# Second attention of a two-block kernel: the query tiles of a pair of heads in the order 0, 7, 1, 6, 2, 5, 3, 4 instead of 0 to 7

## The chip, the core and the metric

One Trainium2 chip, one core. The metric is the device time of one execution in microseconds (us), the median of three runs. Instructions are issued in program order on each engine: TensorE (PE in the rows, PEld its weight loads), VectorE (DVE), ScalarE (ACT), GpSimd (POOL), and SyncE (SP), which issues most transfers. Engines meet through counting semaphores only.

## The reference, cut to what matters

The program is a chain of two transformer blocks over 1024 tokens of width 1024. The second block's attention is causal, with 8 heads of width 64 and a forget bias:

```python
for i in range(S // Q_BLOCK):            # 8 query tiles of 128 rows
    q_blk = q[:, :, q0:q1]
    k_blk = k[:, :, :q1]                 # keys 0 .. q1: tile i has (i + 1) * 128 columns
    logits = einsum('bhqd,bhkd->bhqk', q_blk, k_blk) * scale
    logits = logits + c[:, :, q0:q1, None] - c[:, :, None, :q1]
    p = softmax(where(mask, logits, -inf))
    outs.append(einsum('bhqk,bhkd->bhqd', p, v_blk))
```

Afterwards the result `b_out` is normalised over its 512 columns by row, put beside the gating result, and multiplied with `w_out`. Query tiles do not depend on one another, so their order is free.

## The kernel before

**Items and batches.** The class `Attention` is used twice. For the second attention (`maps == 1`) its list `items` has 64 entries (head, tile): for each of the four pairs of heads, tiles 0 to 7, and for each tile both heads one after the other. I call the two items of one tile a and b. An item of tile i has (i + 1) * 128 score columns. Its probabilities are turned (transposed) and multiplied with the values in batches of up to four 128-column blocks, so that tiles 0 to 3 have one batch for each item and tiles 4 to 7 have two.

**TensorE** (`pe`, L1511 on). Before an even item n it computes the scores of both items of the next tile, n + 2 and n + 3 (`pe_scores`, L1466, with the causal mask added by L1473). Then for each batch b of item n it turns batch b + 1 (`pe_turn`, L1484) and multiplies batch b (`pe_pv`, L1498). So the last turn of item n + 1 is that of the first batch of item n + 2, and that one waits for the exponentials of n + 2. The scores of a head's item fill two of the eight PSUM banks, banks 0 and 1 for a and 2 and 3 for b; new scores wait until the maxima of the tile before are taken (`max0`). No tile further ahead than the next can therefore be under way.

**VectorE** (`dve`). For each item n: `dve_max(n + 2)` (L1589: scores plus bias into `ex`, with the row maximum, and L1592, its negative), the even batches out of PSUM (`evacuate`, L1540), and `dve_out(n)` (L1610, L1617: the result times one over the row sum).

**ScalarE** (`act`). For each item n: the odd batches out of PSUM, `act_exp(n + 2)` (L1552), and what `act_beside_att2` puts there: squares for the normalisation that follows (L2143). The squares of the attention's own results are taken in the last pair of heads, tile by tile, two items after the tile.

```python
if n + 2 < len(self.items) and (self.wide(n + 2) if self.maps == 2 else n % 2 == 0):
    self.pe_scores(pe, n + 2)
for b in range(self.first[n], self.first[n + 1]):
    ...
    if b + 1 < len(self.batches):
        self.pe_turn(pe, b + 1)
    self.pe_pv(pe, b)
```

**After it.** GpSimd makes a root from each square (`pool_m_root`), VectorE scales tile by tile from 0 to 7 (`dve_m_scale`), TensorE turns the scaled tiles and `pe_out` multiplies them with `w_out`, again from tile 0 to 7.

Of the kernel before, what the change touches and what calls it, by code (L numbers as in the profile page):

```python
# [26 lines left out]
NT = SEQ // P  # L27
# [15 lines left out]
NSLOT = 12  # L43
NRAW = 4
NH1, NH2 = 4, 8
LAM_INIT = 0.8 - 0.6 * math.exp(-0.3 * 0)
NEG = -1.0e30
RSQRT_MAGIC = 0x5F3759DF
# [18 lines left out]
def _program(nc, io, ctx):  # L67
# [3 lines left out]
    def sem(name):  # L71
        if name not in sems:
            sems[name] = ctx.enter_context(nc.semaphore(name))
        return sems[name]
# [447 lines left out]
    def loaded(eng, name, n=1):  # L522
        eng.wait_ge(sem("in_" + name), 16 * n)
# [27 lines left out]
    N1 = NT + 1  # L551
# [827 lines left out]
    class Attention:  # L1379
# [7 lines left out]
        def __init__(self, tag, q, k, v, out, heads, dv, meta, maps, ex, atb, bias=None, neglam=None):  # L1387
            self.tag, self.q, self.k, self.v, self.out = tag, q, k, v, out
            self.heads, self.dv, self.meta, self.maps = heads, dv, meta, maps
            self.ex, self.atb, self.bias, self.neglam = ex, atb, bias, neglam  # L1390
            if maps == 2:
                self.items = [(h, i) for h in range(heads) for i in range(NT)]
            else:

                self.items = [(h, i) for g in range(0, heads, 2) for i in range(NT) for h in (g, g + 1)]
            names = ("s0", "s1", "max0", "max1", "exp0", "exp1", "prob", "turned", "evac0", "evac1", "pv",
                     "o_out")
            self.s = {n: sem(f"{tag}_{n}") for n in names if maps == 2 or n not in ("s1", "max1", "exp1", "prob")}

            self.batches = []  # L1400
            for n, (h, i) in enumerate(self.items):
                full = [(meta + t * P, P, t + (1 if meta else 0)) for t in range(i + 1)]
                tiles = full + ([(0, meta, 0)] if meta else [])
                for b in range(0, len(tiles), 4):
                    self.batches.append((n, tiles[b:b + 4]))
            self.first = {}
            for b, (n, _) in enumerate(self.batches):
                self.first.setdefault(n, b)
            self.first[len(self.items)] = len(self.batches)
            self.beside_long = {b for n in range(len(self.items)) if self.items[n][1] == NT - 3  # L1410
                                for b in self.steps(n)}
# [159 lines left out]
        def dve_max(self, v, n, link):  # L1571
            w = self.ncols(self.items[n][1])
            h = self.items[n][0]
            for m in range(self.maps):
                v.wait_ge(self.s[f"s{m}"], n + 1)
                if n >= 3:
                    v.wait_ge(self.s[f"exp{m}"], n - 2)
                if self.maps == 2:
                    if n >= 3:
                        v.wait_ge(self.s["turned"], self.first[n - 2])  # L1580
                    v.tensor_tensor_reduce(self.ex[:, n % 3, m, 0:w], self.score(n, m, 0, w), maskrow[:, L1 - w:L1],  # L1581
                                           -1.0, 3.0e38, ALU.add, ALU.min, negmax[:, n % 3, m:m + 1])\
                        .then_inc(self.s[f"max{m}"], 1)
                else:
                    if self.items[n][1] == 0:
                        v.wait_ge(tile_in[h], 32)
                    if n >= 3:
                        v.wait_ge(self.s["turned"], self.first[n - 2])
                    link(v.tensor_tensor_reduce(self.ex[:, n % 3, 0, 0:w], self.score(n, 0, 0, w),  # L1589
                                                self.bias[:, h, 0:w], 1.0, -3.0e38, ALU.add, ALU.max,  # L1590
                                                lmax[:, n % 2, 0:1]))
                    v.tensor_scalar(negmax[:, n % 3, 0:1], lmax[:, n % 2, 0:1], -1.0, None, ALU.mult)\  # L1592
                        .then_inc(self.s["max0"], 1)
# [527 lines left out]
    att2 = Attention("att2", q2, k2, v2, o2, NH2, ST, 0, 1, ex2, at2, bias=negc)  # L2121
# [8 lines left out]
    m_sq, m_rooted = sem("turn_m_sq"), t1_rooted  # L2130
# [2 lines left out]

    def act_m_square(act, i, part):

        n = i if part else NT + i
        if n:
            act.wait_ge(m_sq, n)
        if not part:
            act.wait_ge(att2.s["o_out"], len(att2.items) - 2 * NT + 2 * i + 2)  # L2140
        src = au[:, i, :] if part else o2[:, :, i * P:(i + 1) * P]
        junk = junk_m[:, :] if part else junk_m[:, :].rearrange("p (k c) -> p k c", k=4)
        nc.scalar.activation(junk, src, ACT.Square, accum_out=stat[:, i, part:part + 1]).then_inc(m_sq, 1)  # L2143

    def act_beside_att2(act, n):

        if n < 4 * NT and n % 4 == 3:
            act_m_square(act, n // 4, 1)
        last = n - (len(att2.items) - 2 * NT)
        if last >= 3 and last % 2 == 1:  # L2150
            act_m_square(act, (last - 3) // 2, 0)

    def pool_m_root(pool, i, part):
        n = i if part else NT + i
        pool.wait_ge(m_sq, n + 1)
        nc.gpsimd.tensor_scalar(tmpa[:, i, part:part + 1], stat[:, i, part:part + 1], 1.0 / HALF, EPS,
                                ALU.mult, ALU.add).then_inc(root_eps, 1)
        eps_added[0] += 1
        pool.wait_ge(root_eps, eps_added[0])
        nc.gpsimd.tensor_tensor(rst[:, i, part:part + 1], tmpa[:, i, part:part + 1], mhalf[:, 0:1], ALU.pow)\  # L2160
            .then_inc(m_rooted, 1)

    def dve_m_scale(v, i):
        for part in range(2):
            v.wait_ge(m_rooted, N1 + (i if part else NT + i) + 1)
            if i >= 2:
                v.wait_ge(m_turned, 2 * (i - 2) + part + 1)
            if part:
                dst, src, gain = xs_m[:, i % 2, 1, :], au[:, i, :], gb_m[:, 0:HALF]
            else:  # L2170
                dst, gain = (t.rearrange("p (k c) -> p k c", k=4) for t in (xs_m[:, i % 2, 0, :], gb_m[:, HALF:D]))
                src = o2[:, :, i * P:(i + 1) * P]
            v.scalar_tensor_tensor(dst, src, rst[:, i, part:part + 1], gain, ALU.mult, ALU.mult).then_inc(m_scaled, 1)
# [424 lines left out]
    @block.gpsimd  # L2598
    def _(pool):
        pool_in1(pool)  # L2600
        pool.wait_ge(met, 3 * K["ssm"])
        pool_weights(pool, U_GLU, U_O1[1])
        for i in range(NT):
            pool_o_root(pool, i)
        pool_y_sums(pool)
        pool_weights(pool, U_O1[1], U_O1[1] + 4)
        pool_y_root(pool)
        pool_weights(pool, U_O1[1] + 4, N_BLOCK1)
        pool_beside_out(pool, 0, mlp1)
        mlp1.pool(pool)  # L2610
        mlp1.freed(pool, 3)
        pool_weights(pool, N_BLOCK1, N_BLOCK1 + 4)
        mlp1.pool_down_lo(pool, NF - 1)
        mlp1.freed(pool, 5)
        u = N_BLOCK1 + 4
        for i in range(NT + 2):
            for k in range((2, 1, 1)[i] if i < 3 else 0):
                pool_weights(pool, u, u + 1)
                u += 1
            if i < NT:  # L2620
                post[1].pool_root1(pool, i)
            if i >= 2:
                post[1].pool_root2(pool, i - 2)
        mlp1.down_over(pool)
        pool_weights(pool, u, len(stream) - 4)
        for part in (1, 0):
            for i in range(NT):
                pool_m_root(pool, i, part)
        pool_weights(pool, len(stream) - 4, len(stream))
        pool_beside_out(pool, 2, mlp2)  # L2630
        mlp2.pool(pool)
        mlp2.pool_down_lo(pool, NF - 1)
        for i in range(NT):
            post[3].pool_root1(pool, i)
# [86 lines left out]
    def _(act):  # L2721
# [87 lines left out]
        load(act, "gb_m", gb_m[:, 0:HALF], rowb(gains_a))  # L2809
        load(act, "gb_m", gb_m[:, HALF:D], rowb(gains_b))  # L2810
        att2.act(act, act_beside_att2)
        act_m_square(act, NT - 1, 0)
        for i in range(NT + 2):
            if i < NT:
                act_m_hi(act, i)
# [12 lines left out]
    def _(v):  # L2828
# [28 lines left out]
        link(v.tensor_tensor(lamv[:, 4:5], lamv[:, 3:4], lamv[:, 2:3], ALU.subtract))  # L2857
        link(v.tensor_scalar(lamv[:, 4:5], lamv[:, 4:5], -LAM_INIT, None, ALU.add))
        dve_ssm_turned(v, link)
# [9 lines left out]
        loaded(v, "gb_o")  # L2869
        link(v.tensor_scalar(gb_o[:, :], gb_o[:, :], 1.0 - LAM_INIT, None, ALU.mult))  # L2870
        for i in range(2):
# [143 lines left out]
```

## Time and profile before

| what | us |
|---|---|
| median of three runs | 2594.71 (2590.66 to 2598.65) |
| the profiled execution, its own time | 2594.34 |
| its span in the trace | 2592.5 |
| mean granted TensorE clock, share of full | 0.973 |
| TensorE matmuls busy | 2426.4 (94%) |
| VectorE, ScalarE, GpSimd busy | 1474.3, 798.0, 1150.1 |
| second attention, from about 1597 to 1762 | 165 |

The chain of work that ended last is 81% TensorE. The first number of a timeline's row is counted from the start of the span. The ends of matmuls are modelled, and each is longer than the distance to the next, so that a group of matmuls is best measured from its start to the start of the next group.

### The profile page before, as it was taken

To read this page: it belongs to the slowest core of one execution; us is meant where nothing else is said; L and a number is where in the kernel's file an instruction comes from. 1 tells how busy PE (TensorE), PEld (TensorE's weight loads), DVE (VectorE), ACT (ScalarE), POOL (GpSimd) and SP (SyncE) were. 2 spreads that over 40 slices of the span, in tenths; PEclk is the share of its full clock that TensorE was granted. 3 is DMA by queue.
4 is the path that set the end of the run, shared out by engine and by line. 5 is a ranking of instruction groups with operands and counts; after the bars stand their busy time and mean duration, and the time that the engine had idled before them with its cause. 6 is when DMAs were issued, how large, how long until landed. Compare 5 with 4: busy or idle time off the path is not lost.

```text
span 2592.5 us, 32813 instructions
## 1 busy us (share of the span) xinstructions
PE 2426.4 (94%) x11718; PEld 1967.5 (76%) x11718; DVE 1474.3 (57%) x2113; ACT 798.0 (31%) x1517; POOL 1150.1 (44%) x888
## 2 busy tenths in 40 slices
PE   7997877898999999999989998989989999999996
PEld 7976755686788888888768886768768888888885
DVE  5974666537456555655574311664645655555556
ACT  4231355624322222222242002552532222222222
POOL 3220040254555555665583443001745565555553
PEclk9998899898999999999999999999999999999998
DMA  5445520023111111211152113001311111111114
GB/s 144 126 130 132 169 73 1 1 81 122 37 49 49 50 59 49 60 49 49 59 181 67 45 54 106 1 1 41 123 41 58 57 53 49 49 49 50 59 49 146
DMA packets 176915, 179.29 MB, mean 69 GB/s; under 512 B 39704, under 2 KB 139544, under 8 KB 176816
## 3 DMA queue, kind: packets, MB, share of 16 engines
q1 hardware_dynamic: 171520, 164.02, 20.9%
q10 hardware_dynamic: 5296, 13.96, 1.5%
q8 instruction: 60, 0.98, 0.2%
q14 instruction: 39, 0.32, 0.0%
HBM read 147.46 MB, written 30.49 MB: 69 GB/s over the span
## 4 chain that ended last, share of the span: by engine, by line
PE 81%; DVE 8%; ACT 4%; issue 2%; DMA 2%; POOL 2%; SPq 0%; POOLq 0%; ACTq 0%; DVEq 0%
PE ps L267 23%; PE ps L268 23%; PE ps L269 23%; PE ps L1498 3%; PE ps L1466 3%; PE ps L1484 2%; ACT ex L1552 2%; PE ps L474 1%; DVE hbuf L425 1%; DMA msb<-ssm_lags 1%; DVE ex L1603 1%; DVE hbuf L1989 1%; PE ps L2710 1%; PE ps L456 0%; DVE hbuf L431 0%
## 5 line engine op out<-in xcount | busy, mean ns | idle before, releaser
L1989 DVE TENSOR_TENSOR hbuf<-hbuf,ps 128x1024 f32<-128x1024 f32 x320 | 390.7, 1221 | 254.0 <-PE ps L269 232.2
L267 PE MATMUL ps<-mlp_dh,mlp_fh 128*128 128x512 f32 x672 | 264.4, 393 | 12.8 <-POOL mlp_dzl L1790 10.0
L269 PE MATMUL ps<-mlp_dh,mlp_fl 128*128 128x512 f32 x672 | 263.3, 392 | 0.0
L268 PE MATMUL ps<-mlp_dl,mlp_fh 128*128 128x512 f32 x672 | 262.7, 391 | 0.0
L207 POOL TENSOR_TENSOR wgt<-raw,ones 128x512 fp32r<-128x512 f32 x76 | 86.7, 1141 | 328.3 <-PE ps L269 165.1
L1777 POOL TENSOR_TENSOR mlp_s_raw<-mlp_gh_raw,mlp_s_raw 128x512 f32<-128x512 f32 x44 | 57.1, 1299 | 284.1 <-PE ps L269 284.1
L267 PEld LDWEIGHTS ps<-mlp_dh,mlp_fh 128*128 128x128 f32 x672 | 126.6, 188 | 43.7 <-POOL mlp_dzl L1790 10.8
L269 PEld LDWEIGHTS ps<-mlp_dh,mlp_fl 128*128 128x128 f32 x672 | 126.5, 188 | 27.7
L268 PEld LDWEIGHTS ps<-mlp_dl,mlp_fh 128*128 128x128 f32 x672 | 126.7, 189 | 27.5
L1790 POOL TENSOR_TENSOR mlp_dl<-mlp_d_raw,mlp_dh 128x1024 fp32r<-128x1024 f32 x42 | 113.9, 2712 | 46.5 <-ACT mlp_dh L1966 46.5
L1484 PE MATMUL ps<-ident,ex 128*128 128x128 f32 (+1 forms) x464 | 83.0, 291 | 41.6 <-DVE ex L1603 26.6
L2026 DVE TENSOR_TENSOR mlp_fl<-mlp_p,mlp_fh 128x512 fp32r<-128x512 f32 x42 | 114.4, 2725 | 3.6
L1552 ACT ACTIVATE ex<-ex,negmax 128x144 f32<-128x144 f32 (+15 forms) x128 | 99.4, 778 | 33.2 <-DVE negmax L1592 32.4
L1777 POOL TENSOR_TENSOR mlp_s_raw<-mlp_gl_raw,mlp_ul 128x512 f32<-128x512 f32 x44 | 57.2, 1300 | 116.0 <-PE ps L269 116.0
L209 POOL TENSOR_TENSOR wgt<-raw,wgt 128x512 fp32r<-128x512 f32 x76 | 104.1, 1370 | 6.0
L1466 PE MATMUL ps<-k,q 64*128 64x512 f32 (+6 forms) x416 | 89.9, 543 | 10.8 <-DVE negmax L1581 7.5
L1484 PEld LDWEIGHTS ps<-ident,ex 128*128 128x128 f32 (+1 forms) x464 | 52.2, 147 | 56.7 <-DVE ex L1603 34.5
L1589 DVE CUSTOM_DVE_ANT_0 ex<-ps,negc 128x128 f32<-128x128 f32 (+7 forms) x64 | 48.2, 754 | 79.4 <-PE ps L1473 79.1
L267 PE MATMUL ps<-x1h,chunk_w 128*128 128x352 f32 (+2 forms) x256 | 89.1, 348 | 2.6 <-DVE x1l L625 1.8
L1923 ACT CAST mlp_s3h<-mlp_s_raw 128x512 fp32r<-128x512 f32 x44 | 27.3, 621 | 202.7 <-POOL mlp_s_raw L1777 202.7
L269 PE MATMUL ps<-x1h,chunk_w 128*128 128x352 f32 (+2 forms) x256 | 87.5, 342 | 0.0
L268 PE MATMUL ps<-x1l,chunk_w 128*128 128x352 f32 (+2 forms) x256 | 87.4, 341 | 0.0
(485 smaller groups left out, 6719.4 us busy)
## 6 DMA issues: line engine op xcount, KB each, us to landing
h<-hbuf SPq DMA_DIRECT2D x24, 512.0 KB, 2.9
mlp_d_raw<-in_w_down SPq DMA_DIRECT2D x21, 512.0 KB, 3.4
mlp_d_raw<-in_w_ffn_out SPq DMA_DIRECT2D x21, 512.0 KB, 3.6
raw<-in_w_in SPq DMA_DIRECT2D x40, 256.0 KB, 2.8
raw<-in_w_out SPq DMA_DIRECT2D x32, 256.0 KB, 2.7
res_b<-h SPq DMA_DIRECT2D x16, 512.0 KB, 4.4
mlp_ul<-in_w_up SPq DMA_DIRECT2D x22, 256.0 KB, 3.0
mlp_uh_raw<-in_w_up SPq DMA_DIRECT2D x22, 256.0 KB, 3.3
```

The costliest lines, as they stand in the source:

```text
L207: nc.gpsimd.tensor_tensor(wh[:, s, :], r, ones[:, 0:1].broadcast_to([P, 512]), ALU.mult).then_inc(w_hi, 1)
L209: nc.gpsimd.tensor_tensor(wl[:, s, :], r, wh[:, s, :].bitcast(F32), ALU.subtract).then_inc(w_split, 1)
L267: pe.matmul(out, lhs[0], rhs[0], start=first, stop=False, skip_group_check=over)
L268: pe.matmul(out, lhs[0], rhs[1], start=False, stop=False, skip_group_check=over)
L269: return pe.matmul(out, lhs[1], rhs[0], start=False, stop=last, skip_group_check=over)
L1466: mm = pe.matmul(self.score(item, m, a, b), self.q[rows, t, i * P:(i + 1) * P], self.k[rows, t, a:b], start=True, stop=True)
L1484: t = pe.transpose(ps[0:w, self.tbank(b), j * P:(j + 1) * P], self.ex[:, n % 3, 0, c:c + w], ident[:, :])
L1552: nc.scalar.activation(e, e, ACT.Exp, scale=-1.0 if self.maps == 2 else 1.0, bias=negmax[:, n % 3, m:m + 1], accum_out=psum_l[:, n % 3, m: ...
L1777: nc.gpsimd.tensor_tensor(blk[name][2][:, :, :], x[:, :, :], y[:, :, :], op).then_inc(self.s["sums"], 1)
L1790: nc.gpsimd.tensor_tensor(self.d[z][1][:, :], self.d_raw[z][:, :], self.d[z][0][:, :].bitcast(F32), ALU.subtract).then_inc(self.s["split"], 1)
L1989: v.tensor_tensor(self.acc[:, i, :], self.acc[:, i, :], src, ALU.add).then_inc(self.s["added"], 1)
L2026: v.tensor_tensor(self.f[b][1][:, c], src, self.f[b][0][:, c].bitcast(F32), ALU.subtract)\
```

## The change

`items` of the second attention runs over the tiles in the order `ORDER2`; the pairing of heads stays. The rest of the diff keeps counts in step with it: the wait of `dve_max` for a head's bias sits at the first tile in the order (still tile 0), and the squares and roots of the attention's result are made and counted in the new order. The stage after it still goes through tiles 0 to 7.

```diff
+ORDER2 = [0, 7, 1, 6, 2, 5, 3, 4]
@@
-                self.items = [(h, i) for g in range(0, heads, 2) for i in range(NT) for h in (g, g + 1)]
+                self.items = [(h, i) for g in range(0, heads, 2) for i in ORDER2 for h in (g, g + 1)]
@@
-                    if self.items[n][1] == 0:
+                    if self.items[n][1] == ORDER2[0]:
                         v.wait_ge(tile_in[h], 32)
@@ def act_m_square(act, i, part):
-        n = i if part else NT + i
+        n = i if part else NT + ORDER2.index(i)
@@
-            act.wait_ge(att2.s["o_out"], len(att2.items) - 2 * NT + 2 * i + 2)
+            act.wait_ge(att2.s["o_out"], len(att2.items) - 2 * NT + 2 * ORDER2.index(i) + 2)
@@ def act_beside_att2(act, n):
-            act_m_square(act, (last - 3) // 2, 0)
+            act_m_square(act, ORDER2[(last - 3) // 2], 0)
@@ def pool_m_root(pool, i, part):
-        n = i if part else NT + i
+        n = i if part else NT + ORDER2.index(i)
@@ def dve_m_scale(v, i):
-            v.wait_ge(m_rooted, N1 + (i if part else NT + i) + 1)
+            v.wait_ge(m_rooted, N1 + (i if part else NT + ORDER2.index(i)) + 1)
@@ gpsimd
-            for i in range(NT):
+            for i in range(NT) if part else ORDER2:
                 pool_m_root(pool, i, part)
@@ scalar
-        act_m_square(act, NT - 1, 0)
+        act_m_square(act, ORDER2[-1], 0)
```

## Rows read from the trace of the kernel before

**Rows 1.** Windows: length, busy of PE, PEld, DVE, ACT, POOL, granted clock, DMA.

```profile
1597.00:1762.00 165.00, 146.19 (x1160) 117.62 (x1160) 108.58 (x369) 84.35 (x207) 18.31 (x37) 0.99 0.09 33
1613.74:1653.44 39.70, 35.39 (x282) 28.41 (x282) 27.16 (x93) 20.91 (x52) 2.97 (x8) 1.00 0.00 1
```

**Rows 2.** Waits of TensorE in one period of the second attention, total, times, longest.

```profile
PE ps L1484 <- ACT ex L1552: 3.5, 4, 1.0
PE ps L1498 <- DVE at L1540: 0.8, 2, 0.6
```

**Rows 3.** Timeline of TensorE: start, duration, line; in brackets the idle time before.

```profile
1643.52 0.28 PE L1484 MATMUL ps<-ident,ex 128*128 128x128 f32 x1
...
1644.97 0.44 PE L1484 MATMUL ps<-ident,ex 128*128 128x128 f32 x2 [1.00 <-ACT ex L1552]
...
1648.17 0.55 PE L1484 MATMUL ps<-ident,ex 128*128 128x128 f32 x3 [0.91 <-ACT ex L1552]
...
1654.77 0.61 PE L1484 MATMUL ps<-ident,ex 128*128 128x128 f32 x4
1655.21 1.00 PE L1498 MATMUL ps<-av,at 128*128 128x64 f32 x8
1656.95 0.66 PE L1484 MATMUL ps<-ident,ex 128*128 128x128 f32 x4 [0.73 <-ACT ex L1552]
```

**Rows 4.** Timeline of VectorE: the first maxima of tiles 4 and 7.

```profile
1654.92 0.82 DVE L1589 CUSTOM_DVE_ANT_0 ex<-ps,negc 128x640 f32<-128x640 f32 x1 [0.98 <-PE ps L1473]
...
1672.44 1.23 DVE L1589 CUSTOM_DVE_ANT_0 ex<-ps,negc 128x1024 f32<-128x1024 f32 x1 [1.39 <-PE ps L1473]
```

**Rows 5.** Timeline of ScalarE: the exponentials of the same items.

```profile
1655.97 0.83 ACT L1552 ACTIVATE ex<-ex,negmax 128x640 f32<-128x640 f32 x1
...
1673.90 1.15 ACT L1552 ACTIVATE ex<-ex,negmax 128x1024 f32<-128x1024 f32 x1 [0.59 <-DVE negmax L1592]
```

**Rows 6.** Timeline of TensorE: waits inside tiles 4 and 5, and around tile 7's scores.

```profile
1662.42 1.08 PE L1498 MATMUL ps<-av,at 128*128 128x64 f32 x8 [0.59 <-DVE at L1540]
...
1668.41 1.07 PE L1498 MATMUL ps<-av,at 128*128 128x64 f32 x8 [0.26 <-DVE at L1540]
...
1672.30 0.50 PE L1484 MATMUL ps<-ident,ex 128*128 128x128 f32 x3
```

**Rows 7.** Waits of TensorE in the stage after the second attention.

```profile
PE ps L267 <- DVE mal L2206: 0.5, 1, 0.5
PE ps L267 <- POOL wgt L209: 0.3, 1, 0.3
```

**Rows 8.** Timeline of TensorE in the first attention: its long idle gaps.

```profile
336.95 0.66 PE L1484 MATMUL ps<-ident,ex 128*128 128x128 f32 x4 [2.75 <-DVE ex L1603]
...
351.71 0.66 PE L1484 MATMUL ps<-ident,ex 128*128 128x128 f32 x4 [1.89 <-DVE ex L1603]
...
377.14 0.66 PE L1484 MATMUL ps<-ident,ex 128*128 128x128 f32 x4 [2.30 <-DVE ex L1603]
...
391.08 0.66 PE L1484 MATMUL ps<-ident,ex 128*128 128x128 f32 x4 [1.89 <-DVE ex L1603]
...
393.14 1.11 PE L1484 MATMUL ps<-ident,ex 128*128 128x128 f32 x4
394.05 1.80 PE L1498 MATMUL ps<-v,at 128*128 128x128 f32 x8
```

**Rows 9.** Windows behind these four gaps; the granted clock is the first number after POOL.

```profile
337.60:341.00 3.40, 2.96 (x11) 1.41 (x11) 0.87 (x4) 2.96 (x7) 3.32 (x4) 0.50 0.23 82
352.00:355.00 3.00, 3.00 (x27) 2.74 (x26) 1.76 (x8) 2.26 (x8) 2.84 (x4) 1.00 0.23 79
378.60:381.90 3.30, 3.02 (x8) 1.48 (x10) 1.45 (x4) 2.19 (x6) 0.00 (x0) 0.50 0.00 0
392.30:395.60 3.30, 3.30 (x15) 2.96 (x15) 1.06 (x4) 1.74 (x8) 0.00 (x0) 0.50 0.00 0
```

## Prediction

> **What bounds the kernel now.** I read the chain of work first: it is TensorE nearly throughout, so what counts is where TensorE idles. Then I cut the second attention out by windows. It takes 165 us; one pair of heads, tiles 0 to 7, takes 39.70 us, with TensorE busy for 35.39 of them at a granted clock of 1.00 [rows 1]. Four pairs of heads run the same pattern, the later two full periods with the same sums. So 39.70 - 35.39 = 4.31 us of a period is idle TensorE, and the reader is to see in the waits what ends it: four waits for the exponentials of the next tile, 3.5 us, and two for a copy out of PSUM, 0.8 us [rows 2]. VectorE (27.16 us) and ScalarE (20.91 us) are far from full; they matter by their latency alone. In the stage behind, TensorE waits for less than 1 us in all [rows 7], so there is no slack there in which a later end of the attention would vanish.
>
> **The change part by part.** No instruction is added or removed: the same 64 items, the same shapes, the same DMAs. Every tile still makes two batches (tiles 0 to 3) or four (4 to 7) for its two heads, always an even number, so each batch keeps its evacuating engine. What changes is which tile's exponentials are awaited behind which tile's matmuls.
>
> Take a step from tile i to tile j. Clock zero is the end of j's scores and mask on TensorE, which is the start of the turn that follows. Until TensorE can turn j, three things happen in a row: VectorE takes the maximum of j, ScalarE its exponentials, TensorE is released. Call this latency L(j). Under it lie only the turn of item i b and the values of item i a, if i has one batch each; call this the cover C(i). If i has two batches each, the cover is all of the long item's turns and values, and no wait is seen in the rows at such a step for j = i + 1; for a shorter j it holds the more.
>
> L from the rows: from 1643.52 to 1644.97 is L(1) = 1.45, from 1654.77 to 1656.95 is L(4) = 2.18 [rows 3]. For tile 7 there is no exposed wait, so I add it up: its turn-side zero is 1672.30 [rows 6], the maximum starts at 1672.44 [rows 4], the exponential at 1673.90 [rows 5], that is 1.60 after zero. Tile 4's turn starts 1656.95 - 1655.97 = 0.98 after its exponential of 0.83 us, 0.15 more than the duration [rows 3, 5], so tile 7's follows 1.15 + 0.15 = 1.30 after: L(7) = 2.90. The line through L(1) and L(4) climbs 0.243 for each tile and gives 2.91, so the two ways agree; it also gives L(5) = 2.42 and L(6) = 2.67.
>
> C from the rows: L less the idle time. C(0) = 1.45 - 1.00 = 0.45 and C(3) = 2.18 - 0.73 = 1.45 [rows 3]; a third of the difference for each tile, 0.33: C(1) = 0.78, C(2) = 1.12.
>
> Now the steps. In rising order the exposed ones are 0-1, 1-2, 2-3 and 3-4: 1.00, then 0.91 and 0.82 by these formulas, 0.73: 3.46 us, which is the 3.5 of [rows 2]. In the new order they are 0-7: 2.91 - 0.45 = 2.46; 1-6: 2.67 - 0.78 = 1.89; 2-5: 2.42 - 1.12 = 1.30; 3-4: 0.73 as now. Sum 6.38. The steps 7-1, 6-2, 5-3, and 4-0 into the next pair of heads, come behind long tiles and are covered, but they were covered before (4-5, 5-6, 6-7, 7-0), so nothing is gained there. The two copy waits, 0.59 in tile 4 and 0.26 in tile 5 [rows 6], lie between the b item's own turn and its own values, and stay. So a pair of heads gains 6.38 - 3.46 = 2.92 us of idle time, four pairs **11.7 us**.
>
> Costed at nothing: the wait for new scores behind a long j. The second maximum of tile 7 can begin some 1.75 us after the first (first maximum 1.23, its negative, the result of item a) and is through near 3.35 us after zero; TensorE reaches the next scores after the turn (some 0.5) and the values of i b (some 0.25) at about 3.65. The cover is 0.3 us; if it is gone, each of three steps costs some tenths, at most 3 us in all. The squares on ScalarE in the last pair of heads keep their places. Roots and scaling: tile 4's root now comes last and is needed fifth rather than eighth by VectorE, after four tiles of output matmuls, and tile 0's, which starts that stage, is ready earlier than all. The last pair of heads ends with tile 4 and its waits instead of tile 7: estimated under 0.3 us either way. The head's bias is waited for at tile 0 in both orders and is loaded as a whole row, so tile 7 coming early waits for no DMA.
>
> **The clock.** The gaps grow from at most 1.0 us to 2.46 and 1.89 us, and such gaps exist in the first attention. There the granted clock went to half (1.2 GHz) behind the gaps of 2.75 and 2.30 us and behind one of 1.89; behind the other gap of 1.89 it held at 2.4 GHz [rows 8, 9]. The pattern of 2.30 recurs twice and that of 391.08 once in the following heads, each with a fall. So I expect three or four falls behind the four gaps of step 0-7 and two behind the four of step 1-6: 5.5. A fall lasted some 3.3 us in these windows [rows 9]. In it four turns took 0.91 us from start to start, which at full clock take 1655.21 - 1654.77 = 0.44 [rows 3, 8]: twice as long. If everything doubles, a fall costs half of 3.3, 1.7 us. The values have 64 columns here and are about half of the work; no row shows them at half clock. Bounds: they double too (1.7 us), or they do not slow at all, being bound by the weight loads (then 3.3 us hold values at full pace and the rest at double, a loss of a third, 1.1 us). I take the middle, 1.4: 5.5 x 1.4 = **7.7 us**. Behind the gap TensorE has a long tile's work without a wait, so nothing absorbs it.
>
> The Trainium skill ("TensorE: Matmul & The Clock Gate", section "Why this matters for your kernels") warns only of idle gaps longer than any forecast here; by it the clock would hold and the sum would end at the bubbles alone. The rows of the first attention speak against it.
>
> **Sum.** 2594.34 (the profiled execution; the median of the runs shown is 2594.71, so no correction) + 11.7 + 7.7 = 2613.7, say **2614 us**, +0.75%.
>
> **The rivals.**
> - *The gaps come, the clock holds.* For it: one gap of 1.89 us passed without a fall, and these gaps are single, where in the first attention smaller ones stood near them. Against it: all gaps above 2.2 us there fell. 2594.3 + 11.7 = 2606 us. Chance 0.19.
> - *The clock falls behind all eight gaps, or twice behind some, and the scores also wait.* 8 x 1.7 = 13.6; 2594.3 + 11.7 + 13.6 = 2620 us or a little more. Chance 0.10.
> - *The order does nothing to the time.* A long tile's surplus cover would have to lie over the next step's latency, so that only sums count. The two-bank scores of each head speak against it: no tile beyond the next is started. 2594 us. Chance 0.05.
> - *Faster.* The long tile placed ahead of a short one lets VectorE and ScalarE run ahead, so that the short tiles' waits vanish (3.46 us for each pair of heads) and the long tiles' latency is met under the preceding work too. It decides if the four exposed gaps together fall below 3.46 us, that is if L(7) were covered by more than 2 us rather than 0.45. At the most 4 x 3.46 = 13.8 us, 2580 us. The wait of new scores for `max0` excludes nearly all of it. Chance 0.03.
> - The forecast itself: 0.63, with a range of its own of 2609 to 2618 (three falls at 1.1 us to seven at 1.7).
>
> **How the numbers follow.** Runs of before lie 4 us to either side of their median, so about 0.3% (8 us) is what can be told from no change. The forecast, the held clock and the many falls are all beyond it: 0.92, of which I give 0.02 to a held clock that is measured low. Slower 0.90, same 0.07, faster 0.03. The range of 8 in 10 must take in the held clock at 2606 and the many falls: 2603 to 2621 leaves out the last two rivals and the edges.
>
> **What will show it.** In a period of the changed kernel: four waits of L1484 for `ex` of about 2.5, 1.9, 1.3 and 0.7 us in place of 1.0 to 0.7; a period of some 42.6 us where the clock is at 1.00, longer by one to two for each fall; windows at a clock of 0.50 right behind steps 0-7 and 1-6 and none behind 2-5 and 3-4; no new wait of L1466 for `negmax`. Busy time of VectorE and ScalarE unchanged; the stage behind the same length, only later. The prediction is wrong if those four waits come out shorter, because something else covers L(7); if waits appear behind the long tiles or before the scores; or if the clock falls also behind the shorter gaps and stays down.

## The result, and the profile after

The changed kernel takes 2613.55 us (median of six runs, 2610.96 to 2622.09) against 2595.55 us before (six runs, 2590.66 to 2598.65). The ratio is 1.0078, with a 95% interval of 1.0058 to 1.0098: slower by 18 us, where 2614 was forecast. The profiled execution took 2614.03 us.

The engines' line on the page of the changed kernel, whose span is 2612.2 us: TensorE is busy 15 us longer than before with the same number of instructions, the other engines hardly change.

```profile
PE 2441.1 (93%) x11718; PEld 1980.9 (76%) x11718; DVE 1476.7 (57%) x2113; ACT 798.9 (31%) x1517; POOL 1150.3 (44%) x888
```

The timeline of TensorE in the changed kernel, one pair of heads: the turns that wait for a tile's exponentials, the idle time in brackets. Turns are L1485 here, values L1499. They answer to [rows 3].

```profile
1651.49 0.66 PE L1485 MATMUL ps<-ident,ex 128*128 128x128 f32 x4 [2.44 <-ACT ex L1553]
...
1662.49 0.66 PE L1485 MATMUL ps<-ident,ex 128*128 128x128 f32 x4 [1.87 <-ACT ex L1553]
...
1674.67 0.66 PE L1485 MATMUL ps<-ident,ex 128*128 128x128 f32 x4 [1.30 <-ACT ex L1553]
...
1685.03 0.66 PE L1485 MATMUL ps<-ident,ex 128*128 128x128 f32 x4 [0.73 <-ACT ex L1553]
...
1706.67 0.66 PE L1485 MATMUL ps<-ident,ex 128*128 128x128 f32 x4 [1.87 <-ACT ex L1553]
```

The reader is to see steps 0-7, 1-6, 2-5 and 3-4, and then 1-6 of the next pair of heads, 44.18 us after its forerunner, where a period was 39.70 before [rows 1]. The waits of TensorE over the whole attention of the changed kernel, total, times, longest, answer to [rows 2]:

```profile
PE ps L1485 <- ACT ex L1553: 26.5, 17, 2.4
PE ps L1499 <- DVE at L1541: 3.4, 8, 0.6
```

The same view of the kernel before has 15.0 and 3.4 us. So the waits for exponentials grew by 11.5 us and the copy waits not at all. Windows of the changed kernel; the granted clock is the first number behind POOL. They answer to [rows 9].

```profile
1605.90:1609.30 3.40, 3.40 (x17) 2.63 (x17) 1.82 (x9) 1.24 (x2) 0.00 (x0) 0.50 0.43 161
1649.00:1652.30 3.30, 0.86 (x9) 0.75 (x8) 2.89 (x9) 1.80 (x4) 0.00 (x0) 1.00 0.00 0
1660.50:1663.80 3.30, 1.43 (x12) 1.21 (x12) 2.86 (x10) 2.18 (x4) 0.00 (x0) 1.00 0.00 0
1663.90:1667.30 3.40, 3.40 (x18) 2.62 (x15) 1.05 (x5) 1.21 (x5) 0.00 (x0) 0.50 0.00 0
1667.40:1670.70 3.30, 3.30 (x32) 3.10 (x30) 2.23 (x8) 1.55 (x4) 0.00 (x0) 1.00 0.02 5
1752.70:1762.80 10.10, 10.10 (x49) 9.35 (x49) 3.31 (x12) 3.11 (x10) 1.49 (x4) 0.50 0.00 1
1600.50:1782.80 182.30, 152.39 (x1115) 122.62 (x1115) 108.28 (x364) 83.72 (x206) 13.45 (x32) 0.93 0.04 16
```

Behind the gap of 1.87 us the clock is at half for 3.4 us, and TensorE, never idle, gets 18 matmuls done where the next window of about the same length, with similar but not the same work, has 32. The first window stands behind step 0-7 of the first pair of heads, the only step of this kind with a fall. In the last pair of heads the clock stays at half for 10.1 us. For the comparisons below I take one stretch, from the first turn of the attention to the first turn of the scaled tiles behind it: the **stage**. It is 159.97 us before and 182.26 us after, +22.3 us. Its half-clock time I work out from its window as 2 x (1 - clock) x length, good to 2 us: none before, 25 us after.

### The profile page after: what moved, and what is told of

It is laid out like the page before. It is cut to its first block, busy times and chain, and to the rows that moved or that the text cites. A ratio compares the mean times of both kernels' runs of the same rounds, so it can differ in the third digit from the quotient of the medians.

```text
span 2612.2 us, 32813 instructions
## 1 busy us (share of the span) xinstructions
PE 2441.1 (93%) x11718; PEld 1980.9 (76%) x11718; DVE 1476.7 (57%) x2113; ACT 798.9 (31%) x1517; POOL 1150.3 (44%) x888
## 4 chain that ended last, share of the span: by engine, by line
PE 82%; DVE 8%; ACT 3%; issue 2%; DMA 2%; POOL 2%; SPq 0%; POOLq 0%; DVEq 0%; ACTq 0%
PE ps L268 23%; PE ps L269 23%; PE ps L270 23%; PE ps L1499 3%; PE ps L1467 3%; PE ps L1485 2%; ACT ex L1553 2%; PE ps L475 1%; DVE hbuf L426 1%; DVE ex L1604 1%; DVE hbuf L1990 1%; PE ps L1358 1%; PE ps L2711 1%; DVE ex L1590 1%; PE ps L457 0%
## 5 line engine op out<-in xcount | busy, mean ns | idle before, releaser
L1485 PE MATMUL ps<-ident,ex 128*128 128x128 f32 (+1 forms) x464 | 87.0, 301 | 53.3 <-DVE ex L1604 26.8
L1485 PEld LDWEIGHTS ps<-ident,ex 128*128 128x128 f32 (+1 forms) x464 | 55.5, 155 | 68.8 <-DVE ex L1604 35.1
L1467 PE MATMUL ps<-k,q 64*128 64x512 f32 (+6 forms) x416 | 93.5, 562 | 10.9 <-DVE negmax L1582 7.6
```

Of the source, the lines that this page charges most:

```text
L1467: mm = pe.matmul(self.score(item, m, a, b), self.q[rows, t, i * P:(i + 1) * P], self.k[rows, t, a:b], start=True, stop=True)
L1485: t = pe.transpose(ps[0:w, self.tbank(b), j * P:(j + 1) * P], self.ex[:, n % 3, 0, c:c + w], ident[:, :])
```

## The experiments

All ratios are against the kernel before, timed on the same chip as each kernel.

### Filled gaps: `e1_filled`

```diff
 for b in range(self.first[n], self.first[n + 1]):
     if b + 1 < len(self.batches):
+        step = (self.items[n][1], self.items[self.batches[b + 1][0]][1])
+        if self.maps == 1 and step in ((0, 7), (1, 6)):
+            self.bank_free(pe, self.tbank(b + 1), b + 1)
+            for _ in range({7: 32, 6: 22}[step[1]]):
+                pe.matmul(ps[:, self.tbank(b + 1), 0:P], identb[:, :], maskb[:, :], start=True, stop=True)
         self.pe_turn(pe, b + 1)
     self.pe_pv(pe, b)
```

> The changed kernel, with small matmuls of no use in the two long gaps of each pair of heads: 32 before the turn that waits in step 0-7, 22 in step 1-6, sized to end before the awaited exponentials. They fill idle time and delay nothing. My theory (idle gaps 11.7 us, and falls of the clock behind them, some 7 to 9 us): TensorE's clock stays at 1.00 through the second attention, a pair of heads takes 42.6 us in place of 44.2, and the kernel takes about 2606 us, 7 us less than the changed one, 11 more than the one before. Rival (the clock is not what costs; the idle gaps and something behind them do): no change against 2613.5. Rival (the clock falls whatever TensorE does, by the place of the long tile's work): falls stay, 2613.5.

Measured: 2605.44 us, ratio 1.0048 (1.0033 to 1.0062). The stage is 171.27 us, +11.3. Two waiting turns of step 1-6 in the timeline of TensorE, one period apart, then the window of the stage:

```profile
1618.58 0.66 PE L1485 MATMUL ps<-ident,ex 128*128 128x128 f32 x4 [0.65 <-ACT ex L1558]
...
1661.16 0.66 PE L1485 MATMUL ps<-ident,ex 128*128 128x128 f32 x4 [0.65 <-ACT ex L1558]
```

```profile
1602.00:1774.00 172.00, 153.79 (x1333) 125.51 (x1334) 108.79 (x367) 84.31 (x208) 14.01 (x34) 1.00 0.05 19
```

The clock holds, the period is 1661.16 - 1618.58 = 42.58 us, and work of no use has made the kernel 8 us faster. This separates the two terms: the exposed latency alone costs 11.3 us in the stage, the clock the other 11.0 of the changed kernel's 22.3. In one period a fall of 3.4 us costs 44.18 - 42.58 = 1.60 us.

### The same sum in four even gaps: `e2_even_gaps`, `e6_even_filled`, `e7_even_burst`

```diff
-ORDER2 = [0, 7, 1, 6, 2, 5, 3, 4]
+ORDER2 = [0, 4, 1, 5, 2, 6, 3, 7]
```

> Order 0, 4, 1, 5, 2, 6, 3, 7. By L(j) - C(i) the four gaps are 0-4: 1.73, 1-5: 1.64, 2-6: 1.55, 3-7: 1.46, sum 6.38 us, the same sum as in the changed kernel but no gap of 1.89 or more. My theory: 11.7 us of idle time is added all the same, and the clock falls at most once or twice: 2607 to 2610 us. Rival (idle time in sum decides over the clock too): as many falls as in the changed kernel, 2613.5. Rival (a gap depends on the long tile alone, or on the short one alone): four gaps that are not spread within 0.3 us, and another sum.

Measured: 2637.74 us, ratio 1.0173 (1.0156 to 1.019). The gaps of a pair of heads in this kernel's timeline:

```profile
1713.63 0.66 PE L1485 MATMUL ps<-ident,ex 128*128 128x128 f32 x4 [1.73 <-ACT ex L1553]
...
1724.55 0.68 PE L1485 MATMUL ps<-ident,ex 128*128 128x128 f32 x4 [1.63 <-ACT ex L1553]
...
1736.82 0.66 PE L1485 MATMUL ps<-ident,ex 128*128 128x128 f32 x4 [1.54 <-ACT ex L1553]
...
1750.46 0.65 PE L1485 MATMUL ps<-ident,ex 128*128 128x128 f32 x4 [1.45 <-ACT ex L1553]
```

and two of its windows, one behind step 3-7 and the stage:

```profile
1643.20:1656.70 13.50, 13.50 (x65) 11.79 (x65) 3.24 (x15) 3.18 (x10) 0.74 (x2) 0.50 0.00 0
1600.50:1809.00 208.50, 180.48 (x1114) 145.32 (x1114) 108.44 (x364) 83.96 (x205) 13.38 (x32) 0.80 0.04 15
```

The gaps are 1.73, 1.63, 1.54 and 1.45, forecast as 1.73, 1.64, 1.55 and 1.46: latency less cover holds for these four pairs of tiles too. My expectation for the time was wrong by 28 us. I had taken 1.89 us as about the shortest gap that brings the clock down; here it falls behind gaps of 1.45 to 1.73 us and stays down for up to 13.5 us. The stage is 208.6 us, 83 us of it at half clock. The rival that idle time in sum decides was too low as well.

The same order, with 20 small matmuls in each of the four gaps:

```diff
+        step = (self.items[n][1], self.items[self.batches[b + 1][0]][1])
+        if self.maps == 1 and n % 2 == 1 and step[1] == step[0] + 4:
+            self.bank_free(pe, self.tbank(b + 1), b + 1)
+            for _ in range(20):
+                pe.matmul(ps[:, self.tbank(b + 1), 0:P], identb[:, :], maskb[:, :], start=True, stop=True)
```

> Order 0, 4, 1, 5, 2, 6, 3, 7 with 20 small matmuls of no use in each of the four gaps, sized to end before the awaited exponentials. The run of this order without them took 2637.7 us, with the clock at half for some 80 us of the attention. Theory (idle time costs 11.7 us, all the rest is the clock, and the clock falls because of the gaps): clock at 1.00 through the attention, 2606 us, 31 us less. Rival (this order has another cost, in a wait of its own): 2620 or more although the clock holds. Rival (the clock is lowered by the kind of work that follows, not by the gaps): the clock still falls, near 2637.

Measured: 2605.01 us, ratio 1.0055 (1.0041 to 1.007). The window of its stage:

```profile
1600.00:1771.00 171.00, 158.99 (x1435) 130.60 (x1436) 108.44 (x364) 84.22 (x205) 13.41 (x33) 1.00 0.05 18
```

The stage is 171.17 us, within 0.1 us of `e1_filled`: two orders with the same forecast sum of 6.38 us cost the same 11.2 to 11.3 us once the clock is held, and all the rest of the 2637.7 us, some 37 us of the stage, was clock. The Trainium skill, "TensorE: Matmul & The Clock Gate", section "A second HAM failure mode: psum-queue depth-cycling", says that a kernel whose TensorE idles briefly and often between groups of matmuls can see its clock swing down and up again. The trace of `e2_even_gaps` agrees: no gap of its stage above 1.73 us, and 83 of 208 us at half clock. The section of the Trainium skill on idle gaps that the prediction weighed, "Why this matters for your kernels" on the same page, would have let all these gaps pass.

To see what keeps the clock down, 16 small matmuls where nothing waits, inside each long tile:

```diff
+        if self.maps == 1 and n % 2 == 0 and self.batches[b + 1][0] == n:
+            self.bank_free(pe, self.tbank(b + 1), b + 1)
+            for _ in range(16):
+                pe.matmul(ps[:, self.tbank(b + 1), 0:P], identb[:, :], maskb[:, :], start=True, stop=True)
```

> Order 0, 4, 1, 5, 2, 6, 3, 7 with its gaps as they are, and 16 small matmuls of no use inside each long tile, before the turn of item a's second batch, where nothing is waited for. They cost 16 x 0.054 = 0.9 us of TensorE at full clock, 16 times: 14 us. Theory (once down, the clock stays down because a long tile's stretch is turns and 64-column values only, and a burst of dense matmuls lets it rise): falls still come behind the gaps, but last 3.4 or 6.8 us, never 10 to 14; half-clock time falls from some 80 us to under 50, and the 14 us of added work are mostly given back: 2630 to 2640 us. Rival (how long it stays down has nothing to do with the work): 80 us or more at half clock, 2652 or more.

Measured: 2629.94 us, ratio 1.0146 (1.013 to 1.0163), at the lower edge of what was expected; the rival of 2652 us is out. The timeline behind step 3-7, where `e2_even_gaps` had its 13.5 us, and the window of the stage:

```profile
1650.39 0.66 PE L1485 MATMUL ps<-ident,ex 128*128 128x128 f32 x4 [1.45 <-ACT ex L1557]
1650.88 1.44 PE L1499 MATMUL ps<-av,at 128*128 128x64 f32 x8
...
1653.17 1.79 PE L1534 MATMUL ps<-maskb,identb 128*128 128x128 bf16 x16
1654.79 0.61 PE L1485 MATMUL ps<-ident,ex 128*128 128x128 f32 x4
1655.24 1.00 PE L1499 MATMUL ps<-av,at 128*128 128x64 f32 x8
```

```profile
1608.50:1803.50 195.00, 165.15 (x1370) 136.66 (x1370) 108.21 (x364) 83.27 (x206) 13.47 (x33) 0.95 0.04 17
```

The clock still falls behind the gap (the x16 burst takes 1.79 us), but the turn right behind the burst runs at full pace again. Half-clock time falls from 83 to 20 us, and by the ratios the 256 useless matmuls made the kernel some 7 us faster. All six falls in this trace last 3.4 us; in that of `e2_even_gaps` there are twelve, and five of them last 10.2 or 13.7 us. So in this trace, with dense bursts, the clock comes back sooner and falls less often. Turns with 64-column values alone can keep it down but do not always: four of the five falls of the changed kernel ended after 3.4 us without a burst. That is as far as it was tested: which of the two, turns or values, holds it down was not tried, and the bursts shift all that follows in time.

### The sum of the old order in one gap: `e3_one_gap`

```diff
-ORDER2 = [0, 7, 1, 6, 2, 5, 3, 4]
+ORDER2 = [0, 7, 6, 5, 4, 3, 2, 1]
```

> Order 0, 7, 6, 5, 4, 3, 2, 1. Gaps by L(j) - C(i): 0-7 2.46, 3-2 0.24, 2-1 0.33, and 1-0 into the next pair of heads 0.42: sum 3.45, that of the kernel before, but in one long gap. Since tile 1 comes last and its root is wanted second, about 1.2 us are added at the end. My theory: idle time as before, and two to four falls of the clock behind step 0-7 at 1.6 us: 2595.5 + 1.2 + 3 to 6 = 2600 to 2603 us. Rival (idle time alone counts, no clock): 2596 to 2597 us. Rival (alternation of long and short is what costs, not the steps' gaps): no loss, 2595.5.

Measured: 2605.37 us, ratio 1.0041 (1.0025 to 1.0056), 11 us where 5 to 8 were expected. The gaps are 2.44, 0.44, 0.45 and 0.46 us. The waits of TensorE say that the idle time as a whole hardly moved (15.9 against 15.0 us); the window of the stage shows the clock. The last block has ScalarE, VectorE and TensorE in step 3-2:

```profile
PE ps L1485 <- ACT ex L1553: 15.9, 16, 2.4
...
PE ps L2180 <- DVE xs_m L2174: 1.3, 2, 1.1
```

```profile
1606.70:1777.00 170.30, 150.96 (x1114) 118.84 (x1114) 108.29 (x363) 83.63 (x205) 13.31 (x32) 0.94 0.05 19
```

```profile
1725.15 0.58 ACT L1541 COPY at<-ps 128x512 f32<-128x512 f32 x1 [1.34 <-PE ps L1485]
1725.25 0.15 DVE L1593 TENSOR_SCALAR negmax<-lmax 128x1 f32<-128x1 f32 x1
1725.63 0.62 ACT L1553 ACTIVATE ex<-ex,negmax 128x384 f32<-128x384 f32 x1
1726.39 0.55 PE L1485 MATMUL ps<-ident,ex 128*128 128x128 f32 x3 [0.44 <-ACT ex L1553]
```

The three short gaps are longer than forecast (0.24, 0.33 and 0.42), and these rows say why. Tile 2's maximum is ready at 1725.40, but ScalarE is still copying the last batch of the longer tile 3 out of PSUM, and its exponential starts at 1725.63, when the copy is about done. From the end of the scores, 1724.51, to the turn it is 1.88 us, where L(2) was 1.69 in rising order (1646.48 to 1648.17 in the kernel before), 0.19 more and so nearly all of the difference. In rising order the maximum of the longer tile takes longer than that copy, and the exponential waits for it. So the latency of a short tile behind a longer one also depends on the tile before it.

About 20 us at half clock, in the profiled execution at all four gaps of step 0-7, make most of the 10.5 us by which the stage is longer. The rivals that idle time alone counts, or that only alternation costs, are out. The delay of the scaled tiles was over-estimated: TensorE waits there hardly longer than in the changed kernel (1.1 us once).

### Values before the waiting turn: `e4_values_first`, `e9_first_again`, `e5_values_first_new`

```diff
+    early = self.maps == 1 and n % 2 == 1 and self.first[n + 1] - self.first[n] == 1
+    if early:
+        self.pe_pv(pe, b)
     if b + 1 < len(self.batches):
         self.pe_turn(pe, b + 1)
-    self.pe_pv(pe, b)
+    if not early:
+        self.pe_pv(pe, b)
```

In rising order:

> The rising order of the kernel before; where item b of a tile has one batch, TensorE multiplies its values before it turns the next tile's first batch, not behind that wait. By my theory a gap is latency less cover, and the cover grows by these values: 0.26, 0.48, 0.71, 0.93 us for tiles 0 to 3. Gaps: 0-1 0.74, 1-2 0.43, 2-3 0.11, 3-4 none; 3.46 falls to 1.28, 2.2 us for a pair of heads, 8.7 us in all: 2587 us. Rival (the values then wait for ScalarE's copy of their own turned batch, and the wait only moves): waits of L1499 for `at` come up for what the others lose, 2595 us. Rival (ScalarE's exponentials come later since its copy is awaited sooner): no gain or a loss.

Measured: 2588.12 us, ratio 0.998 (0.9967 to 0.9993). The waits of TensorE in its stage:

```profile
PE ps L1499 <- DVE at L1545: 3.4, 8, 0.6
PE ps L1485 <- ACT ex L1557: 2.5, 5, 1.1
PE ps L1499 <- ACT at L1545: 1.6, 8, 0.3
```

15.0 us of waits for exponentials have become 2.5, and 1.6 us of waits for ScalarE's copy are new, as the first rival had it in kind but not in size. The stage is 152.20 us, 7.8 us shorter, for 8.7 forecast. The waits in sum fell by 10.9 us, more than the stage did. Starts tell where the rest is. In step 0-1:

```profile
1642.32 0.28 PE L1485 MATMUL ps<-ident,ex 128*128 128x128 f32 x1
...
1643.78 0.44 PE L1485 MATMUL ps<-ident,ex 128*128 128x128 f32 x2 [0.32 <-ACT ex L1557]
1644.14 0.92 PE L1467 MATMUL ps<-k,q 64*128 64x384 f32 x4
```

From turn to turn it is 1.46 us, as before (1.45, [rows 3]): the latency has not moved. What is saved stands behind the waiting turn: the next scores start 0.36 us after it, where they started 0.54 us after it (1644.97 to 1645.51) in the kernel before. That is 0.18 us, and 0.26 was forecast. The waits in brackets make it look like more, since they are counted from the modelled ends, and part of the latency now lies under the end of one more group of matmuls. A period, start to start, is the safer measure: a pair of heads takes 37.75 us here and 39.70 before, 1.95 us less, where 2.2 was forecast.

Its second run:

> Rising order with values first, once more, beside its variant with split batches on the same chip. By the traces its attention stage is 7.8 us shorter than before (152.2 us against 160.0). If the stage is all: 0.3% under the kernel before, 2587 us. If the distance of 10.7 us between the two variants' medians (two calls) was a property of the kernels, this one comes out 10 us above the other; if it came from the calls and from stages that the variants share, 2 to 4 us above.

Measured: 2585.14 us, ratio 0.9958 (0.9944 to 0.9973), beside 2582.47 for `e10_split_again`, 3 us apart, which the two intervals do not separate; 10 us did not come again. In this profiled execution the stage took 155.66 us with a granted clock of 0.97, though the code is that of the 152.20 us. The longest wait of the stage in it is the one at its start, and a fall comes 1.6 us after it. (Every kernel here also waits 5.5 to 6.8 us for a transfer ahead of the stage; in this trace that wait ended 6.2 us before the one shown did.)

```profile
1606.89 0.33 PE L1486 MATMUL ps<-ident,ex 128*128 128x128 f32 x1 [1.15 <-ACT ex L1558]
...
1608.50:1618.70 10.20, 10.03 (x39) 6.60 (x39) 5.31 (x24) 4.52 (x14) 1.07 (x3) 0.50 0.52 205
```

The same wait of 1.15 us stands in `e4_values_first` and in the kernel before, with no fall in the stage: the clock falls in some executions of a kernel and not in others, and at the start of the stage it can do so behind a gap that short.

In the changed order:

> The order of the changed kernel with the values of a one-batch item b multiplied before the waiting turn. By latency less cover the gaps are 0-7 2.46 - 0.26 = 2.20, 1-6 1.89 - 0.48 = 1.41, 2-5 1.30 - 0.71 = 0.59, 3-4 none, and about 0.3 us of waits for the copy that the run in rising order showed behind tiles 0 and 1: 4.5 us for a pair of heads against 6.4, so 7 to 8 us less than the changed kernel, and one or two falls of the clock fewer, 1.6 us each: 2602 to 2606. Rival (the bubbles do not add up from latency less cover; the order as such costs 18 us): the same 6 or 7 us gained as in rising order, but the distance of the two orders stays 18 us: 2606 to 2607.

Measured: 2601.2 us, ratio 1.0031 (1.0018 to 1.0044), which is 8 us above the kernel before, as expected; runs from 2591.78 to 2609.56. The timeline of its steps 0-7, 1-6 and 2-5, and of the copy waits ahead of the first two:

```profile
1658.06 0.41 PE L1499 MATMUL ps<-av,at 128*128 128x64 f32 x2 [0.28 <-ACT at L1545]
1660.23 0.66 PE L1485 MATMUL ps<-ident,ex 128*128 128x128 f32 x4 [1.76 <-ACT ex L1557]
...
1669.35 0.63 PE L1499 MATMUL ps<-av,at 128*128 128x64 f32 x4 [0.16 <-ACT at L1545]
1671.06 0.66 PE L1485 MATMUL ps<-ident,ex 128*128 128x128 f32 x4 [1.08 <-ACT ex L1557]
...
1681.26 0.66 PE L1485 MATMUL ps<-ident,ex 128*128 128x128 f32 x4 [0.41 <-ACT ex L1557]
...
1701.23 0.66 PE L1485 MATMUL ps<-ident,ex 128*128 128x128 f32 x4 [1.76 <-ACT ex L1557]
```

The time of the whole kernel does not decide against the rival: by the ratios this order is 0.0051 above `e4_values_first`, 13 us, but 0.0073 above the second run of the same code, `e9_first_again`, 19 us. The periods at full clock do. A pair of heads takes 1701.23 - 1660.23 = 41.00 us here and 42.58 in `e1_filled`; in rising order it takes 37.75 with values first and 39.70 without. So the order costs 3.25 us a pair with values first and 2.88 without, 13.0 and 11.5 us in all. By latency less cover it is 2.92 in both cases: the added cover takes as much from either order. Values first save 1.6 us a pair here, where 1.9 was forecast. What the order costs beyond 13 us in an execution is the clock's. The spread of the runs goes with the clock too: the shortest has a mean clock of 0.974, the longest 0.968. The profiled execution, 2609.56 us, is the longest of them, and all of its fall is one stretch at the start:

```profile
1611.50:1628.60 17.10, 16.57 (x72) 13.38 (x73) 5.87 (x20) 4.87 (x13) 0.74 (x2) 0.50 0.17 62
1628.70:1779.40 150.70, 132.60 (x1027) 104.88 (x1026) 99.38 (x338) 77.38 (x190) 10.40 (x28) 1.00 0.00 1
```

### The copy waits: `e8_first_split`, `e10_split_again`

```diff
-for b in range(0, len(tiles), 4):
-    self.batches.append((n, tiles[b:b + 4]))
+size = 3 if maps == 1 and i in (4, 5) else 4
+for b in range(0, len(tiles), size):
+    self.batches.append((n, tiles[b:b + size]))
```

> Rising order, values first, and the batches of tiles 4 and 5 split 3 and 2, and 3 and 3 blocks, rather than 4 and 1, and 4 and 2. The waits of 0.59 and 0.26 us for the copy of item b's first batch lie between that batch's turn and its values; the shorter first and longer second batch make the copy 0.13 us shorter and the cover 0.2 to 0.4 us longer. Expected waits 0.3 and 0: 0.5 us for a pair of heads, 2 us in all, 2586 us; more than can be told from the clock of the whole kernel, but to be seen in the waits. Rival (the copies then collide with VectorE's next maximum): waits as before or longer, 2588 or above.

Measured: 2577.39 us, ratio 0.9946 (0.9934 to 0.9959). The waits of TensorE in its stage:

```profile
PE ps L1486 <- ACT ex L1558: 2.5, 5, 1.1
PE ps L1500 <- ACT at L1546: 1.5, 7, 0.3
```

The waits for VectorE's copy, 3.4 us in `e4_values_first` as in the kernel before, are gone rather than more than halved. But that is 3.4 us, not the 10.7 by which the medians of the two variants differ, which were timed on different chips. So I ran both again on one chip:

> Rising order, values first, tiles 4 and 5 in batches of 3 and 2 and of 3 and 3, once more. The stage is 150.1 us in its trace, 9.9 us under the kernel before; 2 to 4 us under the variant without the split. Expected 0.4% under the kernel before, 2584 to 2585 us; if the 15 us of its first run were real, 2578.

Measured: 2582.47 us, ratio 0.9952 (0.9936 to 0.9968), 3 us under `e9_first_again`, with runs from 2573.16 to 2590.03; the stage is 148.90 us, 11.1 under before. The whole times alone do not tell the split from its absence. The periods do: a pair of heads takes 36.93 us here and in `e8_first_split`, and 37.75 without the split, 3.3 us in all, the 3.4 of the waits. This is the version with the shortest stage: 0.5% under the kernel before and 1.3% under the changed one, by the ratios.

## Why the prediction was right

**The gaps.** Forecast 2.46, 1.89, 1.30 and 0.73; measured 2.44, 1.87, 1.30 and 0.73. The sum of 11.7 us for the attention was 11.5 in the waits and 11.3 in the stage with the clock held (`e1_filled`). Five further gaps, the four shown of `e2_even_gaps` and the long one of `e3_one_gap`, came within 0.02 us of the same formula. Where it misses is told above: by 0.04 to 0.2 us when a short tile follows a longer one, whose copy holds up ScalarE, and by some 0.2 us where values are moved before the wait. No exposed step of the changed kernel is of either kind.

**The cover that was costed at nothing.** No wait of L1467 for `negmax` is in the list of waits, and the copy waits are unchanged. TensorE waits for the scaled tiles 1.1 us once, as before. Both steps were right.

**The clock.** That it would fall behind the long gaps and cost several us was right; the size was low, the places were partly wrong, and the rule by which the falls were counted did not hold. Forecast were three or four falls behind step 0-7 and two behind 1-6, 7.7 us. The profiled execution shows the fall behind 1-6 in all four pairs of heads and behind 0-7 in the first alone, though the windows above have TensorE less busy around the gap of 2.44 us that passed (0.86 us) than around the gap of 1.87 us that did not (1.43 us): the length of the gap alone does not decide, nor how busy TensorE is around it. In `e3_one_gap` the clock was at half at the same gap in four of four places. Five falls where 5.5 were forecast is therefore in good part luck: the count took gaps from 1.89 us on, and in `e2_even_gaps` twelve falls came behind gaps of 1.42 to 1.73 us. A fall of 3.4 us cost 1.60 us, not 1.4. The bound to take was the upper one, since the values double like the rest; a group at half clock in the changed kernel's last pair of heads, eight matmuls from 1753.50 to 1755.10, 1.60 us, against 0.84 at full clock (1610.53 to 1611.37 in the same trace):

```profile
1753.50 1.81 PE L1499 MATMUL ps<-av,at 128*128 128x64 f32 x8
1755.10 1.06 PE L1485 MATMUL ps<-ident,ex 128*128 128x128 f32 x4
```

And one fall lasted 10.1 us, where the prediction gave each some 3.3 us. That was to be read in the trace of before: the window of [rows 9] behind the gap of 2.75 us ends at 341.00, but the clock does not rise there. The next window, TensorE alone:

```profile
341.00:344.41 3.41, 3.41 (x17) 0.50 0.28 77
```

In all the clock cost 11.0 us of the stage in this one execution, where 7.7 were forecast. Two of the six runs took 2622 us at a mean clock of 0.964, against 0.967 in the profiled one, so others pay more.

**The sum.** 11.3 + 11.0 = 22.3 us, where the prediction had 19.4. The medians are 18 us apart. The two profiled executions are 19.7 us apart in their spans: in the changed one the attention's first turn came 2.3 us earlier (1600.54 against 1602.80), in a part that the change does not touch. Over all the profiles that first turn lies between 1597.68 and 1608.53 us. So the last 3 us of the agreement are luck; what was understood is the 11 us of latency, and that the clock adds to it, with about two thirds of what it did add.

**The rivals.** The held clock (2606 us) is what `e1_filled` made true, at 2605.4. The rule of the Trainium skill on idle gaps ("TensorE: Matmul & The Clock Gate", "Why this matters for your kernels"), by which it would have come by itself, does not hold for this kernel: the clock fell behind gaps of 1.87 us. The rival in which nothing is gained or lost by the order, and the faster one, fall with the gaps. The rival of falls behind all eight long gaps, 2620 us, did not come here, with five falls; `e2_even_gaps`, with twelve at its sixteen gaps, went 18 us beyond it.

## What to carry to other kernels

Where one engine works a stage ahead of the others, cost an order of unequal tiles step by step: the next tile's latency less what the present tile leaves to be done under it. A long tile's surplus was worth nothing behind it here, where the buffers admit one tile of lookahead, so a short tile should be followed by a tile as short as can be; no run tried more lookahead. Idle time in gaps of 1.5 to 2.5 us cost as much again through TensorE's clock in the changed kernel, and three times as much in `e2_even_gaps`: look at the granted clock in narrow windows before an order is trusted, and first try to move ready work in front of the waiting instruction (7.8 us here); small matmuls in the gap are a second best.

## What the runs showed of the hardware

- The granted clock fell to half behind gaps of 1.42 to 1.73 us in `e2_even_gaps`, where the prediction went by 1.89 us and more, and stayed there for up to 13.5 us while TensorE was busy without a break with turns, values of 64 columns and a few scores. In one execution (`e9_first_again`) it fell behind a wait of 1.15 us at the start of the stage. A burst of 16 bf16 matmuls of 128 columns was followed by full clock (`e7_even_burst`).
- The cost of half clock in the stage: 11.0 us for some 25 us in the changed kernel, 37.4 us (208.6 - 171.2) for 83 us in `e2_even_gaps`: close to half of the time, so hardly anything is hidden under it.
- Executions of one and the same kernel differ in it: 17.1 us at half clock in one of `e5_values_first_new`, whose runs spread over 18 us; none and about 10 us in two of the rising order with values first.
